# A second, packed table of powers for the outputs of a state-space mixer, stored by GpSimd beside the full one

## The chip, the cores and the metric

One core of one Trainium2 chip. The metric is device time in microseconds for one execution. The kernel before took 4363.01 us in the median of three runs (4361.12 to 4366.87).

## The reference, cut to what matters

Two blocks of a diffusion-style transformer run one after the other on 512 latent and 256 context tokens of width 1024, all in 32-bit floats. The last mixer is a diagonal state-space model over 128 groups of 16 channels with 64 complex states each, run in both directions:

```python
lam = lax.complex(lam_re, lam_im)
dt = jnp.exp(log_step)[:, None]
abar = jnp.exp(lam * dt)
bbar = ((abar - 1.0) / lam)[..., None] * bmat
...
h[t] = abar * h[t - 1] + bbar @ u[t]
y[t] = (c @ h[t]).real
```

The kernel works in chunks of 8 tokens. A chunk's outputs are what its inputs give inside the chunk (a Toeplitz block) plus the entering state times C times the powers 1 to 8 of `abar` in one direction, and the powers in the other order in the backward one. So C times nine powers of `abar` (0 to 8) is a table. The kernels (Toeplitz rows) need powers 0 to 7, the outputs need 1 to 8.

## The kernel before, in words

The whole network is one program of blocks. A block gives each engine its own stream of instructions, and ends when every engine has drained; the next block starts on all engines together. Weights come through a ring of two slots (`c.ring`), loaded by SP.

**The table routine.** `s5_tables` (line 2034) makes the tables for a range of the 16 blocks of channels, wholly on GpSimd, beside the work of other engines in three earlier stages: blocks 0 to 2 in the first attention (lines 941 and 3160), blocks 3 to 10 in the first product of the first feed-forward layer (`dense_seven`, line 360 on, called at 3174 to 3184), and blocks 11 to 15 in the window attention (line 3276). The call is the whole of GpSimd's stream in that block of the program, with its last waits on its own stores. Per block of channels it runs, in this order: six products for direction 0 of the input table, loads for direction 1 (`load_b`, lines 2061 and 2063), the real part of the power table (three products of 1152 columns, `times`, lines 2081 to 2083), its store (`keep_c`, line 2071), six products for direction 1, the store of the input table (line 2108), loads for the next block, a wait until the power table's store has landed, the other part of the power table into the same buffer, its store, six short products for a small table, its store (line 2118), and three loads (lines 2066 to 2068). Every product waits for the one it depends on. GpSimd issues all these transfers itself.

The power table of one block of channels is `[128, part 2, direction 2, pair 4, power 9, channel 16]`, 2304 floats per partition, kept in DRAM as `s5_c9`.

**The mixer.** In `s5_mixer` (line 2125) the rows of the input projection are turned through DRAM, `inputs` makes each chunk's contribution to the states, and `kernels` makes the Toeplitz rows for blocks 0 to 13 early. VectorE then scans the states of both halves of the blocks. After that comes a list of 18 turns, `turn`: the outputs of block 0, kernels 14, outputs 1, kernels 15, then outputs 2 to 15. Turn n uses half n % 2 of the ring, in which GpSimd has loaded the power table (`for_turn`, line 2278, 1152 KB) once turn n - 2 is done (line 2304 and after). After it GpSimd issues eight loads of Toeplitz rows (line 2319). `outputs` on TensorE multiplies 128 of the 144 columns of each of 16 pieces of the table by the entering states (line 2396), then adds the Toeplitz part (line 2403). ScalarE copies the states apart (`part_states`) and the results out, SP stores them, and SP and ScalarE load them back turned.

```python
for n, (kind, b) in enumerate(turn):
    if n >= 2:
        before, of = turn[n - 2]
        pool.wait_ge(y_done if before == "y" else k_done, of + 1)
        for_turn(n)
```

Of the kernel before, what the change touches and what calls it, by code (L numbers as in the profile page):

```python
# [2024 lines left out]
def s5_scratch(c):  # L2025

    dram = lambda name, *shape: c.nc.dram_tensor(name, shape, F32, kind="Internal").ap()
    c.s5 = {"fa": dram("s5_fa", S5_STEP, 2, 128, 128), "pc": dram("s5_pc", 16, 128, 160), "a8": dram("s5_a8", 128, 512),
            "b8": dram("s5_b8", 16, 128, 2048), "c9": dram("s5_c9", 16, 128, 2304), "fb": dram("s5_fb", 16, 128, 512),
            "us": dram("s5_us", 16, 128, T), "ys": dram("s5_ys", 16, 128, LAT), "e": dram("s5_e", 16, 128, 240),  # L2030
            "h": dram("s5_h", 128, KD * LAT), "u": dram("s5_u", 128, KD * LAT)}


def s5_tables(c, pool, spaces, first, end):

    nc = c.nc
    used = [0] * len(spaces)

    def take(*shape):

        n = int(np.prod(shape))
        i = next(i for i, x in enumerate(spaces) if used[i] + n <= x.shape[1])
        v = spaces[i][:, used[i]:used[i] + n]
        used[i] += n
        names = "abc"[:len(shape)]
        return v.rearrange(f"p ({' '.join(names)}) -> p {' '.join(names)}", **dict(zip(names[1:], shape[1:]))) if len(shape) > 1 else v
    bn, fa, b8 = take(2, 512), take(2, 512), take(2, 2, 512)
    prod = take(8, S5_POW, 16)  # L2050
    c9 = take(8, S5_POW, 16)
    cp, pc, bz, fb = take(2, 8, 16), take(160), take(2, 8, 32), take(2, 8, 32)
    tag = f"s5tab{first}_"
    in_b, in_c, made, b8_out, c9_out, fb_out = (c.sem(tag + n) for n in ("in_b", "in_c", "made", "b8_out", "c9_out", "fb_out"))
    tt = nc.gpsimd.tensor_tensor
    n = [0]

    def load_b(b, d):
        for part in range(2):
            rows = c.s5["fa"][:, part, 8 * b + 4 * d:8 * b + 4 * d + 4, :].rearrange("r a y -> r (a y)")  # L2060
            pool.dma_start(fa[:, part, :], rows.unsqueeze(1).broadcast_to([S5_STEP, 16, 512])).then_inc(in_b, 16)
            cols = c.ins["s5_bn"][b, :, 1024 * part + 512 * d:1024 * part + 512 * d + 512]
            pool.dma_start(bn[:, part, :], cols.unsqueeze(0).broadcast_to([S5_STEP, 16, 512])).then_inc(in_b, 16)

    def load_c(b):
        pool.dma_start(cp.rearrange("p a b c -> p (a b c)"), c.ins["s5_cp"][b]).then_inc(in_c, 16)
        pool.dma_start(pc, c.s5["pc"][b]).then_inc(in_c, 16)
        pool.dma_start(bz.rearrange("p a b c -> p (a b c)"), c.ins["s5_bz"][b]).then_inc(in_c, 16)

    def keep_c(b, part):  # L2070
        pool.dma_start(c.s5["c9"][b, :, 1152 * part:1152 * part + 1152], c9.rearrange("p a b c -> p (a b c)")).then_inc(c9_out, 16)

    def step(ins):

        ins.then_inc(made, 1)
        n[0] += 1
        pool.wait_ge(made, n[0])

    def times(out, tmp, re_, im_, a, b, sign):

        tt(out, re_, a, ALU.mult)  # L2081
        step(tt(tmp, im_, b, ALU.mult))  # L2082
        step(tt(out, out, tmp, ALU.add if sign > 0 else ALU.subtract))  # L2083
    def make_b(b, d):

        pool.wait_ge(in_b, 64 * (2 * (b - first) + d + 1))
        flat = prod.rearrange("p a b c -> p (a b c)")[:, 0:512]
        times(b8[:, 0, d, :], flat, bn[:, 0, :], bn[:, 1, :], fa[:, 0, :], fa[:, 1, :], -1)
        times(b8[:, 1, d, :], flat, bn[:, 0, :], bn[:, 1, :], fa[:, 1, :], fa[:, 0, :], 1)
    load_b(first, 0)  # L2090
    load_c(first)
    for b in range(first, end):
        done = b - first
        if done:
            pool.wait_ge(b8_out, 16 * done)
        make_b(b, 0)
        load_b(b, 1)
        pool.wait_ge(in_c, 48 * (done + 1))
        if done:
            pool.wait_ge(c9_out, 32 * done)  # L2100
            pool.wait_ge(fb_out, 16 * done)
        cb = lambda part: cp[:, part].unsqueeze(2).broadcast_to([128, 8, S5_POW, 16])
        pb = lambda part: (pc[:, 72 * part:72 * part + 72].rearrange("p (k e) -> p e k", e=8).unsqueeze(3)
                           .broadcast_to([128, 8, S5_POW, 16]))
        times(c9, prod, cb(0), cb(1), pb(0), pb(1), 1)
        keep_c(b, 0)
        make_b(b, 1)
        pool.dma_start(c.s5["b8"][b], b8.rearrange("p a d n -> p (a d n)")).then_inc(b8_out, 16)
        if b + 1 < end:
            load_b(b + 1, 0)  # L2110
        pool.wait_ge(c9_out, 32 * done + 16)
        times(c9, prod, cb(0), cb(1), pb(1), pb(0), -1)
        keep_c(b, 1)
        fp = lambda part: pc[:, 144 + 8 * part:152 + 8 * part].unsqueeze(2).broadcast_to([128, 8, 32])
        small = prod.rearrange("p a b c -> p (a b c)")[:, 0:256].rearrange("p (a b) -> p a b", a=8)
        times(fb[:, 0], small, bz[:, 0], bz[:, 1], fp(0), fp(1), -1)
        times(fb[:, 1], small, bz[:, 0], bz[:, 1], fp(1), fp(0), 1)
        pool.dma_start(c.s5["fb"][b], fb.rearrange("p a b c -> p (a b c)")).then_inc(fb_out, 16)
        if b + 1 < end:
            load_c(b + 1)  # L2120
    for sem, per in ((b8_out, 16), (c9_out, 32), (fb_out, 16)):
        pool.wait_ge(sem, per * (end - first))


def s5_mixer(c):
# [10 lines left out]
    nc = c.nc  # L2136
# [8 lines left out]
    b8 = [c.view(rest + 2048 * n, 2, 2, 8, 64) for n in range(2)]  # L2145
    toep = [c.view(rest + 1024 * n, 8, 128) for n in range(2)]
    fb = [c.view(rest + 2048 + 512 * n, 2, 2, 4, 32) for n in range(2)]
    band = [c.view(rest + 3072 + 240 * n, 240) for n in range(2)]
    yst = [c.view(rest + 3552 + 512 * n, 512) for n in range(2)]
    powers = lambda x: x.rearrange("p (a d q k) -> p a d q k", a=2, d=2, q=4)  # L2150
    c9 = [powers(c.ring[:, n, 0:2304]) for n in range(2)]
    free = c.hu[:, 0].rearrange("p a b -> p (a b)")
    c9_first = [powers(free[:, 2304 * n:2304 * n + 2304]) for n in range(2)]
    fb_first = [free[:, 4608 + 512 * n:5120 + 512 * n].rearrange("p (a d q n) -> p a d q n", a=2, d=2, q=4) for n in range(2)]
    band_first = [free[:, 5632 + 240 * n:5872 + 240 * n] for n in range(2)]
    NF = 14
    turn = [x for b in range(NB - NF) for x in (("y", b), ("k", NF + b))] + [("y", b) for b in range(NB - NF, NB)]
    place = {x: c9[n % 2] for n, x in enumerate(turn)} | {("k", b): c9_first[b % 2] for b in range(NF)}
    band_of = lambda b: (band_first if b < NF else band)[b % 2]
    fb_of = lambda b: (fb_first if b < NF else fb)[b % 2]  # L2160
    spot = lambda b: c.P[:, 2 * ((b // 2) % 2) + b % 2, 768:1008] if b < NF else bank(4 + b % 2)[:, 0:240]
# [18 lines left out]
    b8_in, c9_in, c9_first_in, fb_in, e_out, t_in, ys_out = (  # L2180
        [S(f"{w}{n}") for n in range(2)] for w in ("b8_in", "c9_in", "c9_first_in", "fb_in", "e_out", "t_in", "ys_out"))
# [26 lines left out]
    with nc.Block() as block:  # L2208
# [42 lines left out]
        def _(pool):  # L2251
# [23 lines left out]

            def for_turn(n):

                pool.dma_start(c9[n % 2].rearrange("p a d q k -> p (a d q k)"), c.s5["c9"][turn[n][1]]).then_inc(c9_in[n % 2], 16)
            load_b8(0)
            load_b8(1)  # L2280
            pool.wait_ge(spilled, 32)
# [20 lines left out]
# [3 lines that stand above are left out]
# [18 lines left out]
        def _(pe):  # L2323
# [60 lines left out]
            def outputs(b):  # L2384

                n = turn.index(("y", b))
                pe.wait_ge(c9_in[n % 2], 16 * (n // 2 + 1))
                if b >= 4:
                    pe.wait_ge(y_kept, b - 3)
                to = [bank(b % 4)[:, 2 * CL * q:2 * CL * (q + 1)] for q in range(4)]  # L2390
                for d in range(2):
                    pe.wait_ge(parted, 2 * b + d + 1)
                    for q in range(4):
                        for part in range(2):
                            of = 16 * (1 - d)
                            last = nc.tensor.matmul(to[q], place["y", b][:, part, d, q, of:of + 128],
                                                    apart[(2 * b + d) % 3][:, part, q].rearrange("p e s -> p (e s)"),
                                                    start=d == 0 and part == 0 and q == 0, stop=False, skip_group_check=True)
                    last.then_inc(apart_used, 1)
                pe.wait_ge(t_in[b % 2], 128 * (b // 2 + 1))  # L2400
                for q in range(4):
                    for e in range(2):
                        last = nc.tensor.matmul(to[q][:, CL * e:CL * (e + 1)], toep[b % 2][:, 2 * q + e, :], up[:, b, 2 * q + e, CX:CH],
                                                start=False, stop=q == 3 and e == 1, skip_group_check=True)
                last.then_inc(y_done, 1)
# [1012 lines left out]
```

## Time and profile before

| | |
|---|---|
| median of three runs | 4363.01 us |
| the profiled execution, time | 4374.75 us |
| the profiled execution, span | 4373.0 us |
| mean granted TensorE clock | 0.95 of full |
| TensorE / VectorE / ScalarE / GpSimd busy | 90 / 58 / 28 / 28% |
| DMA traffic | 532.69 MB, 122 GB/s |

The profiled execution took 11.7 us longer than the median. Busy shares are means over stages that have different limits. A busy TensorE is not TensorE at its peak. `q` behind an engine's name (POOLq) is its sequencer: branches, drains, semaphores and the issue of transfers. The time from issue to landing of a transfer is not part of the instruction's own duration.

### The profile page before, as it was taken

Reading aid. Unit: us, or ns where it says so; the run is one execution under the profiler, and the core shown is the slowest. Engines: PE = TensorE matmul, PEld = TensorE weight load, DVE = VectorE, ACT = ScalarE, POOL = GpSimd, SP = SyncE. Lnnn points to the kernel's source line nnn. Section 1 sums busy time; section 2 is a strip of 40 time slices with the busy share of each in tenths; the row PEclk is TensorE's granted clock in tenths of the full one; section 3 lists DMA queues with packets and bytes.
Section 4 is the critical chain, followed back from the end, with each engine's and each line's share of the span. In section 5 each row is a group of like instructions: output and inputs, shape, how many; then the busy total and the mean of one; then the engine's idle time right before and its main releaser. Section 6 shows DMA issues by size and latency. Waiting matters only on the chain. (4 is left out here: it accounts for less than half of the span.)

```text
span 4373.0 us, 53517 instructions
## 1 busy us (share of the span) xinstructions
PE 3922.7 (90%) x19818; PEld 2826.6 (65%) x19818; DVE 2536.2 (58%) x4524; ACT 1235.2 (28%) x2638; POOL 1214.4 (28%) x1480
## 2 busy tenths in 40 slices
PE   7899899989889777898989999989999789659998
PEld 4577455555445565777878885568755456658886
DVE  6634799982379885557678734245534309823353
ACT  3145311100212474662021102128611211341112
POOL 1174299950000068820000000059600011440000
PEclk9999999999999988999999999999999899889999
DMA  4542366651121066544345422124211276783221
GB/s 172 190 115 78 118 176 187 177 166 60 36 77 58 18 195 176 116 95 165 105 157 174 147 71 76 63 65 111 89 58 53 73 259 197 231 219 117 77 87 67
DMA packets 287391, 532.69 MB, mean 122 GB/s; under 512 B 176960, under 2 KB 184000, under 8 KB 262848
## 3 DMA queue, kind: packets, MB, share of 16 engines
q1 hardware_dynamic: 215872, 343.19, 24.2%
q0 software_dynamic: 53600, 181.04, 14.0%
q10 hardware_dynamic: 17696, 5.56, 0.6%
q8 instruction: 130, 2.13, 0.2%
q14 instruction: 93, 0.76, 0.1%
HBM read 429.55 MB, written 100.01 MB: 121 GB/s over the span
## 5 line engine op out<-in xcount | busy, mean ns | idle before, releaser
L417 PE MATMUL P<-hu,ring 128*128 128x384 f32 (+1 forms) x2448 | 746.3, 458 | 22.2 <-PEq L171 12.1
L417 PEld LDWEIGHTS P<-hu,ring 128*128 128x128 f32 x2448 | 466.8, 191 | 277.8 <-issue 25.6
L653 PE MATMUL P<-area,ring 128*128 128x256 f32 (+1 forms) x1880 | 493.9, 419 | 48.9 <-PEq L393 27.2
L653 PEld LDWEIGHTS P<-area,ring 128*128 128x128 f32 x1880 | 362.5, 194 | 169.7 <-issue 65.3
L417 PE MATMUL P<-area,ring 128*128 128x256 f32 (+1 forms) x1584 | 442.2, 431 | 3.6 <-DVE area L544 2.8
L873 POOL TENSOR_TENSOR fold<-mod,vec 128x16 f32<-128x16 f32 (+1 forms) x5 | 1.0, 206 | 1383.9 <-SPq L852 961.6
L417 PEld LDWEIGHTS P<-area,ring 128*128 128x128 f32 x1584 | 300.5, 190 | 127.6 <-issue 5.3
L653 PE MATMUL P<-area,hu 128*128 128x256 f32 (+1 forms) x1104 | 296.7, 423 | 0.0
L653 PEld LDWEIGHTS P<-area,hu 128*128 128x128 f32 x1104 | 209.8, 190 | 77.2
L2596 DVE SCALAR_TENSOR_TENSOR area<-area 128x1024 f32<-128x1024 f32 x122 | 220.4, 1807 | 19.1 <-ACT area L2672 17.0
L1092 DVE TENSOR_REDUCE stat<-P 128x1 f32<-128x512 f32 (+1 forms) x144 | 99.4, 690 | 151.2 <-PE P L1011 93.0
L2339 PE MATMUL P<-hu,ring 128*128 128x256 f32 (+1 forms) x512 | 169.3, 492 | 15.2 <-PEq L852 15.2
L2083 POOL TENSOR_TENSOR area<-area 128x512 f32<-128x512 f32 (+2 forms) x104 | 180.4, 1735 | 8.2
L1008 PE MATMUL P<-area 128*128 128x256 f32 (+2 forms) x480 | 167.7, 433 | 11.3 <-DMA area<-in_window_mask 5.9
L417 PE MATMUL P<-hu 128*128 128x384 f32 x504 | 170.6, 488 | 5.7 <-DVE hu L529 3.4
L2081 POOL TENSOR_TENSOR area<-area 128x512 f32<-128x512 f32 (+2 forms) x110 | 169.2, 1538 | 19.4 <-DMA area<-in_s_bn 15.7
L2082 POOL TENSOR_TENSOR area<-area 128x512 f32<-128x512 f32 (+2 forms) x104 | 157.4, 1514 | 0.0
L2339 PEld LDWEIGHTS P<-hu,ring 128*128 128x128 f32 x512 | 97.7, 192 | 84.7 <-issue 78.3
L1035 PE MATMUL P<-tmp,area 128*128 128x128 f32 x1152 | 152.4, 275 | 0.1
L879 POOL TENSOR_TENSOR tmp<-tmp 128x768 f32<-128x768 f32 (+1 forms) x6 | 9.3, 1542 | 488.5 <-ACT tmp L904 488.5
L417 PEld LDWEIGHTS P<-hu 128*128 128x128 f32 x504 | 95.0, 190 | 75.6 <-DVE hu L529 6.4
L3086 ACT ACTIVATE tmp<-P 128x768 f32<-128x768 f32 (+1 forms) x44 | 31.0, 704 | 395.2 <-DVE P L549 373.7
(457 smaller groups left out, 7218.6 us busy)
## 6 DMA issues: line engine op xcount, KB each, us to landing
ring<-in_w_ffn_in SPq DMA_DIRECT2D x44, 1024.0 KB, 4.8
area<-in_w_mod SPq DMA_DIRECT2D x69, 512.0 KB, 3.4
ring<-s_c POOLq DMA_DIRECT2D x18, 1152.0 KB, 9.8
stat<-in_w_mod SPq DMA_DIRECT2D x39, 512.0 KB, 3.4
s_c<-area POOLq DMA_DIRECT2D x32, 576.0 KB, 3.4
ring<-in_w_ffn_out SPq DMA_DIRECT2D x24, 704.0 KB, 4.0
area<-s_b POOLq DMA_DIRECT2D x16, 1024.0 KB, 5.4
hu<-s_c POOLq DMA_DIRECT2D x14, 1152.0 KB, 8.9
```

What stands on the lines that cost most here:

```text
L417: last = mm(to, col(a, k), b[:, k, :], start=fresh and k == 0, stop=k == q - 1, skip_group_check=True)
L653: last = mm(to, a[:, 128 * k:128 * k + 128], b[k], start=fresh and k == 0, stop=k == q - 1, skip_group_check=True)
L879: nc.gpsimd.tensor_tensor(sq[0], sq[0], sq[1], ALU.add).then_inc(s["paired"], 1)
L1008: last = nc.tensor.matmul(S[n % 2][:, a:b], q(i, j, t), k(i, j, key, key + b - a), start=True, stop=rope is None and not (edges and key < ...
L1035: last = nc.tensor.matmul(O[n % 2], v(i, j, key), probT[:, n % 2, b * 128:b * 128 + 128], start=b == 0, stop=b == len(tiles) - 1)
L1092: nc.vector.reduce_max(small[:, n % slots, 0:1], scores(n), AX.X).then_inc(sem["top"], 1)
L2081: tt(out, re_, a, ALU.mult)
L2082: step(tt(tmp, im_, b, ALU.mult))
L2083: step(tt(out, out, tmp, ALU.add if sign > 0 else ALU.subtract))
L2339: last = nc.tensor.matmul(c.P[:, 2 * (g % 2) + j, a:b], c.ring[:, s, (j * KD + k) * 128:(j * KD + k + 1) * 128], c.u[:, k, a:b], start=k = ...
L2596: return c.nc.vector.scalar_tensor_tensor(out=junk, in0=weights, scalar=1.0, in1=c.view(CONDS, 2, D)[:, cc % 2, :], op0=ALU.mult, op1=ALU. ...
L3086: return None if j else act_fn(split_tile(tmp[:, 0:w].unsqueeze(1)), split(ps, n), ACT.Silu)
```

## The change

`s5_tables` keeps storing the full table and now stores a second one, `s5_c8`, beside it: for each part, direction 0's powers 1 to 8 and direction 1's powers 0 to 7, as `[128, part, direction, 512]`. That is two more stores after each of the two present ones, each 256 KB, read from the table's buffer as four pieces of 128 floats per partition, written as 512 floats in a row. The semaphore of these stores counts 96 per block in place of 32, in all waits on it. In the mixer the turns of kind "y" load the packed table (1024 KB, 2048 floats per partition) in place of the full one (1152 KB); the turns of kind "k" and the early kernels still load the full one. The matmul of line 2396 takes all 128 columns of a piece in place of 128 of 144.

```diff
--- before.py
+++ after.py
@@ -2026,7 +2026,7 @@
 
     dram = lambda name, *shape: c.nc.dram_tensor(name, shape, F32, kind="Internal").ap()
     c.s5 = {"fa": dram("s5_fa", S5_STEP, 2, 128, 128), "pc": dram("s5_pc", 16, 128, 160), "a8": dram("s5_a8", 128, 512),
-            "b8": dram("s5_b8", 16, 128, 2048), "c9": dram("s5_c9", 16, 128, 2304), "fb": dram("s5_fb", 16, 128, 512),
+            "b8": dram("s5_b8", 16, 128, 2048), "c9": dram("s5_c9", 16, 128, 2304), "c8": dram("s5_c8", 16, 128, 2, 2, 512), "fb": dram("s5_fb", 16, 128, 512),
             "us": dram("s5_us", 16, 128, T), "ys": dram("s5_ys", 16, 128, LAT), "e": dram("s5_e", 16, 128, 240),
             "h": dram("s5_h", 128, KD * LAT), "u": dram("s5_u", 128, KD * LAT)}
 
@@ -2069,6 +2069,9 @@
 
     def keep_c(b, part):
         pool.dma_start(c.s5["c9"][b, :, 1152 * part:1152 * part + 1152], c9.rearrange("p a b c -> p (a b c)")).then_inc(c9_out, 16)
+        for d in range(2):
+            later = c9[:, 4 * d:4 * d + 4, 1 - d:9 - d, :].rearrange("p a b c -> p a (b c)")
+            pool.dma_start(c.s5["c8"][b, :, part, d, :].rearrange("p (a n) -> p a n", a=4), later).then_inc(c9_out, 16)
 
     def step(ins):
 
@@ -2097,7 +2100,7 @@
         load_b(b, 1)
         pool.wait_ge(in_c, 48 * (done + 1))
         if done:
-            pool.wait_ge(c9_out, 32 * done)
+            pool.wait_ge(c9_out, 96 * done)
             pool.wait_ge(fb_out, 16 * done)
         cb = lambda part: cp[:, part].unsqueeze(2).broadcast_to([128, 8, S5_POW, 16])
         pb = lambda part: (pc[:, 72 * part:72 * part + 72].rearrange("p (k e) -> p e k", e=8).unsqueeze(3)
@@ -2108,7 +2111,7 @@
         pool.dma_start(c.s5["b8"][b], b8.rearrange("p a d n -> p (a d n)")).then_inc(b8_out, 16)
         if b + 1 < end:
             load_b(b + 1, 0)
-        pool.wait_ge(c9_out, 32 * done + 16)
+        pool.wait_ge(c9_out, 96 * done + 48)
         times(c9, prod, cb(0), cb(1), pb(1), pb(0), -1)
         keep_c(b, 1)
         fp = lambda part: pc[:, 144 + 8 * part:152 + 8 * part].unsqueeze(2).broadcast_to([128, 8, 32])
@@ -2118,7 +2121,7 @@
         pool.dma_start(c.s5["fb"][b], fb.rearrange("p a b c -> p (a b c)")).then_inc(fb_out, 16)
         if b + 1 < end:
             load_c(b + 1)
-    for sem, per in ((b8_out, 16), (c9_out, 32), (fb_out, 16)):
+    for sem, per in ((b8_out, 16), (c9_out, 96), (fb_out, 16)):
         pool.wait_ge(sem, per * (end - first))
 
 
@@ -2149,13 +2152,14 @@
     yst = [c.view(rest + 3552 + 512 * n, 512) for n in range(2)]
     powers = lambda x: x.rearrange("p (a d q k) -> p a d q k", a=2, d=2, q=4)
     c9 = [powers(c.ring[:, n, 0:2304]) for n in range(2)]
+    c8 = [powers(c.ring[:, n, 0:2048]) for n in range(2)]
     free = c.hu[:, 0].rearrange("p a b -> p (a b)")
     c9_first = [powers(free[:, 2304 * n:2304 * n + 2304]) for n in range(2)]
     fb_first = [free[:, 4608 + 512 * n:5120 + 512 * n].rearrange("p (a d q n) -> p a d q n", a=2, d=2, q=4) for n in range(2)]
     band_first = [free[:, 5632 + 240 * n:5872 + 240 * n] for n in range(2)]
     NF = 14
     turn = [x for b in range(NB - NF) for x in (("y", b), ("k", NF + b))] + [("y", b) for b in range(NB - NF, NB)]
-    place = {x: c9[n % 2] for n, x in enumerate(turn)} | {("k", b): c9_first[b % 2] for b in range(NF)}
+    place = {x: (c8 if x[0] == "y" else c9)[n % 2] for n, x in enumerate(turn)} | {("k", b): c9_first[b % 2] for b in range(NF)}
     band_of = lambda b: (band_first if b < NF else band)[b % 2]
     fb_of = lambda b: (fb_first if b < NF else fb)[b % 2]
     spot = lambda b: c.P[:, 2 * ((b // 2) % 2) + b % 2, 768:1008] if b < NF else bank(4 + b % 2)[:, 0:240]
@@ -2275,7 +2279,9 @@
 
             def for_turn(n):
 
-                pool.dma_start(c9[n % 2].rearrange("p a d q k -> p (a d q k)"), c.s5["c9"][turn[n][1]]).then_inc(c9_in[n % 2], 16)
+                kind, b = turn[n]
+                table = c.s5["c8"][b].rearrange("p a d n -> p (a d n)") if kind == "y" else c.s5["c9"][b]
+                pool.dma_start(place[turn[n]].rearrange("p a d q k -> p (a d q k)"), table).then_inc(c9_in[n % 2], 16)
             load_b8(0)
             load_b8(1)
             pool.wait_ge(spilled, 32)
@@ -2392,8 +2398,7 @@
                     pe.wait_ge(parted, 2 * b + d + 1)
                     for q in range(4):
                         for part in range(2):
-                            of = 16 * (1 - d)
-                            last = nc.tensor.matmul(to[q], place["y", b][:, part, d, q, of:of + 128],
+                            last = nc.tensor.matmul(to[q], place["y", b][:, part, d, q, :],
                                                     apart[(2 * b + d) % 3][:, part, q].rearrange("p e s -> p (e s)"),
                                                     start=d == 0 and part == 0 and q == 0, stop=False, skip_group_check=True)
                     last.then_inc(apart_used, 1)
```

## Rows read from the trace of the kernel before

**Rows 1.** Windows; columns: us, busy (instructions) per engine, PEclk, DMA, GB/s.
```profile
517.00:949.00 432.00, 406.81 (x1240) 236.29 (x1240) 393.13 (x321) 56.47 (x103) 392.29 (x312) 0.98 0.62 183
...
3747.00:3923.00 176.00, 116.80 (x1013) 113.56 (x1008) 96.21 (x202) 68.10 (x116) 88.76 (x152) 0.84 0.81 229
```

**Rows 2.** End of the feed-forward stage, line 393; ns min/median/max, start.
```profile
L393 DVEq COMPARE_BRANCH  x1: 47/47/47, 940.3 to 940.3; - x1
...
L393 POOLq COMPARE_BRANCH  x1: 38/38/38, 944.5 to 944.5; - x1
L393 POOLq DRAIN  x1: 4627/4627/4627, 944.7 to 944.7; - x1
...
L393 PEldq EVENT_SEMAPHORE  x1: 51/51/51, 949.5 to 949.5; - x1
```

**Rows 3.** Waits from 940 to 950 us: us in total, times, longest.
```profile
DVE area L725 <- PEq L393: 9.3, 1, 9.3
```

**Rows 4.** End of the window attention, line 975.
```profile
L975 POOLq DRAIN  x1: 6179/6179/6179, 3138.9 to 3138.9; - x1
...
L975 DVEq DRAIN  x1: 325/325/325, 3145.6 to 3145.6; - x1
```

**Rows 5.** End of the first attention, line 975.
```profile
L975 POOLq DRAIN  x1: 3732/3732/3732, 381.6 to 381.6; - x1
...
L975 DVEq DRAIN  x1: 325/325/325, 416.4 to 416.4; - x1
```

**Rows 6.** Waits in the output turns, 3747 to 3923 us.
```profile
POOL ring L2278 <- PE P L2403: 61.0, 13, 18.6
...
PE P L2396 <- ACT tmp L2427: 29.0, 6, 16.9
PE P L2396 <- DMA ring<-s_c: 24.8, 9, 5.5
```

**Rows 7.** Line 2071, the present stores of the table.
```profile
L2071 POOL DMA_DIRECT2D s_c<-area x32: 600/621/627, 268.2 to 3131.2; - x32
...
DMA to landing us min/median/max: 3.1/3.4/6.6
```

**Rows 8.** Other transfers of GpSimd: lines 1447 and 2256.
```profile
L1447 POOL DMA_DIRECT2D hu<-gdn_xa x8: 565/566/575, 1623.4 to 1659.8; - x8
...
L2256 POOL DMA_DIRECT2D area<-s_b x16: 527/528/579, 3485.5 to 3749.3; - x16
```

**Rows 9.** GpSimd in the feed-forward stage: waits, then in order of time.
```profile
POOL area L2081 <- DMA area<-in_s_bn: 10.3, 4, 6.5
...
528.57 3.00 POOL L2081 TENSOR_TENSOR area<-area 128x512 f32<-128x512 f32 x1 [6.49 <-DMA area<-in_s_bn]
...
553.13 0.62 POOL L2071 DMA_DIRECT2D s_c<-area  x1 [0.30 <-POOL area L2083]
555.45 2.12 POOL L2081 TENSOR_TENSOR area<-area 128x512 f32<-128x512 f32 x1 [1.70 <-DMA area<-in_s_bn]
...
569.58 2.33 POOL L2081 TENSOR_TENSOR area<-area 128x1152 f32<-128x1152 f32 x1
```

**Rows 10.** GpSimd's products of 512 columns: later stages, then first attention.
```profile
L2083 POOL TENSOR_TENSOR area<-area 128x512 f32<-128x512 f32 x52 | 79.3, 1525 | 4.1
...
L2083 POOL TENSOR_TENSOR hu<-hu 128x512 f32<-128x512 f32 x12 | 15.2, 1270 | 0.9
```

**Rows 11.** Line 2118, the store of the small table, 256 KB.
```profile
DMA to landing us min/median/max: 2.4/2.4/4.3
```

**Rows 12.** Line 2278; 3720 to 3762; page: KB, median us to landing.
```profile
DMA to landing us min/median/max: 6.4/9.8/12.6
...
area<-s_b POOLq DMA_DIRECT2D x6, 1024.0 KB, 6.4
ring<-s_c POOLq DMA_DIRECT2D x2, 1152.0 KB, 9.2
...
ring<-in_w_s_in SPq DMA_DIRECT2D x8, 1024.0 KB, 8.9
```

## The prediction

> **What bounds the kernel now.** I read the page first. No engine is full over the span and the chain of the end is only the last layer norm, so the stages must be read one by one. GpSimd and ScalarE have the smallest shares of the span, which says nothing of the stretches where GpSimd makes the tables: in the longest it is busy 392.3 of 432 us [rows 1].
>
> Then I read what ends each stage that runs the table routine, by the drains and branches that close a block. The feed-forward stage (eight tables): VectorE reaches its branch at 940.3, GpSimd at 944.5, GpSimd's drain then takes 4.63 us, and all engines go on at 949.5 [rows 2]. VectorE waited 9.3 us there for that block's end [rows 3]. So **GpSimd ends this stage**. The window attention (five tables): GpSimd's drain runs from 3138.9 for 6.18 us, to 3145.1; VectorE's from 3145.6 to 3145.9 [rows 4]. GpSimd has 0.8 us of slack. The first attention (three tables): GpSimd is through at 381.6 + 3.7 = 385.3, the block closes after VectorE's drain at 416.4 [rows 5], so about 31 us of slack.
>
> Last, the output part of the state-space mixer. TensorE waits there 24.8 us for the power table and 29.0 us for ScalarE's state copies [rows 6]; a table load is issued when the outputs two turns before are done, and GpSimd waits 61.0 us for those [rows 6]. The DMA engines are 81% busy there [rows 1].
>
> **The change, part by part.**
>
> *Four more stores per table, issued by GpSimd.* The present two stores cost 0.62 us each on its queue [rows 7]. The new ones carry 256 KB each, but a row is read as four pieces of 512 B, 512 pieces in all; no GpSimd transfer of before has so many. The nearest rows: a load of 128 pieces takes 0.528 us, one of 192 (line 1447: 32 rows by 6 by 128 B) 0.566 [rows 8], and the present store of 128 rows 0.621 [rows 7]; the count hardly shows. Lower bound: 0.53 us. Upper bound: if the whole 0.566 us went by pieces, 0.566 x 512 / 192 = 1.51 us. I take 0.62, since a store with as many rows is the nearest in kind.
> Whether VectorE stretches an issue: the 32 present stores took 0.600 to 0.627 us [rows 7], also those beside a VectorE that was 393 of 432 us busy [rows 1]. GpSimd's products are stretched there, a 512-column one from 1.27 up to 3.00 us [rows 9, 10], the issues are not. If they were, by the same factor, one would cost 1.46 us (rival 2).
> The Trainium skill (page SBUF — State Buffer, section SBUF: two separate sides) says that GpSimd can't write the descriptors of its transfers while VectorE runs an operation in a two-port mode, and gives about 3.1 us in place of 0.62 for such a transfer; taken as the cost of each of 52 issues that would be an estimate of some +160 us. The trace does not agree for this kernel's stores.
>
> *Feed-forward stage:* 8 x 4 x 0.62 = 19.8 us more on the engine that ends the stage. Part is absorbed: GpSimd waits 10.3 us in four places for the loads of the next product, 6.5 of it once at the start, before any store [rows 9]. The other three, 3.8 us together, come after the first store (the one shown, 1.70 us, begins at 553.75 [rows 9]); two issues ahead of each take away at most 1.24 us each. I take 3. The loads waited for are ahead of the stores in their queue, so the stores don't delay them. And the added time runs after VectorE has ended, where GpSimd's products are quicker: 1.27 us for 512 columns in the first attention, 1.53 in the mean later [rows 10]. The last 20 us of 432 gain some 1.5. Result: 19.8 - 3 - 1.5 = +15.3.
>
> *Window attention:* 5 x 4 x 0.62 = 12.4, less 0.8 of slack: +11.6. There TensorE now stands idle before its next block, and its first products may run at a lower granted clock; 0 to 3 us, I take 1. *First attention:* 3 x 4 x 0.62 = 7.4 us inside 31: nothing. If that cover were gone it would be 7.4.
>
> *The waits on the stores.* After the part-0 stores GpSimd needs the buffer back for part 1. Between lie six products, one store and four loads, 554 to 569.6 in the block shown [rows 9]; the present store lands in 3.4, 6.6 at most [rows 7], and two more of 256 KB at 2.4 to 4.3 each [rows 11] still fit. The second wait has as much cover. What stands behind it, if it is late, is the whole rest of the block. Priced at nothing. The final wait of each call is on the last store of the small table, issued after the new ones; at most 1 us, taken as nothing.
>
> *DMA traffic.* 64 stores of 256 KB, 16.8 MB, 13.6 of them in the two stages that count. Engines that wait for weights there don't end the stage. Nothing.
>
> *Output turns.* 16 of 18 loads shrink from 1152 to 1024 KB. A load lands in 9.8 us in the median [rows 12]. At an equal rate a ninth goes, 1.1 us. Two loads are in flight for two turns, so a turn gains half of that where the table is waited for: about 3 us over outputs 2 to 7; I put 1 for outputs 8 to 15, where the 29.0 us for ScalarE [rows 6] mostly fall. The store of outputs and its way back, for which ScalarE waits, shares the same engines. I take -4; bounds: 0, and what 16 x 128 KB take at the 229 GB/s of the stretch [rows 1], 9 us. The first two tables were loaded early and gain nothing. The matmuls read the same 128 columns: nothing. What is late next is ScalarE's chain of copies.
>
> *Sum:* 15.3 + 11.6 + 1 - 4 = **+24 us**. The profiled execution took 4374.75 (span 4373.0) and would take 4398.7; the median of the runs is 4363.01, 11.7 less than the profiled one, and I carry the same difference over: **4387**.
>
> **The rivals.**
> 1. *The issue goes by pieces.* Then 1.51 instead of 0.62: 48.3 - 3.8 + 30.2 - 0.8 + 1 - 4 = +71, 4434. For it: nothing in the trace has 512 pieces on this queue. Against: 128 and 192 pieces differ by 38 ns, and a present store of 128 takes more than either [rows 7, 8]. It decides if an issue passes 1 us.
> 2. *VectorE stretches the issues* of the feed-forward stage, where it is busiest, to 1.46: 46.7 - 3.8 + 11.6 + 1 - 4 = +51, 4414. For it: the products are stretched. Against: no present store is [rows 7]. (Beside this stands the rule of the Trainium skill's page SBUF — State Buffer, section SBUF: two separate sides.)
> 3. *Most comes back.* Issues at 0.53: 17.0 - 3.8 - 1.5 + 10.6 - 0.8 = 21.5, and the outputs gain their full 9 and the two stage ends, whose drains differ between 3.7 and 6.2 us [rows 4, 5], end 4 earlier together: +8.5, 4371, at the edge of no change.
> 4. *Faster.* The long rows themselves slow the table load, and a load of 1024 KB lands in 5 to 6 us: the other table, of that size, lands in 6.4 where this one takes 9.2 [rows 12]. Place: the output turns, where TensorE's 24.8 us of table waits go, and ScalarE's 29.0 by a third because the stores of outputs find the engines free: -34.5. It decides if that passes the +28 of the table stages: 4363 + 27.9 - 34.5 = 4356. Against: where the engines are busy a 1024 KB load of weights takes 8.9 [rows 12] too, and the fastest table load took 6.4 [rows 12].
> 5. *It doesn't do what it says.* The ring half is no smaller a target, and the same number of loads run; if the landing depends on the number of rows and not on bytes, the outputs gain nothing: +28, 4391. It is inside the forecast's range.
>
> **How the numbers follow.** Forecast with rival 5: 0.73. Rival 1: 0.10. Rival 2: 0.03. Rival 3: 0.09. Rival 4: 0.05. 0.2% is 8.7 us, about what a measurement can tell from no change. Slower takes the forecast and rivals 1 and 2, 0.86; same rival 3, 0.09; faster rival 4, 0.05. Range: the low terms (rival 3 without its earlier ends) give +12.5, so 4375, and I set 4374; upwards the forecast's own bounds (nothing absorbed, clock 3, outputs 0) give +34, 4397, and I go on to rival 2 and an issue of about 1 us, 4414, which holds half of rival 1. Left out: rivals 3 and 4 and half of 1, 0.19.
>
> **What would show it.** Right: four more GpSimd issues of about 0.62 us per table; blocks of the table routine about 2.5 us longer; VectorE's wait at the end of the feed-forward stage up from 9.3 to about 25 us, and some 12 us at the end of the window attention; table loads of 1024 KB landing near 8.7 us. Wrong: an issue near or above 1 us, GpSimd waiting for its own stores, or the feed-forward stage ended by VectorE.

## The result, and the profile after

The changed kernel takes 4394.45 us (median of 3 runs, 4392.08 to 4395.68) against 4363.01: ratio 1.0069 [1.0056, 1.0083], slower. Run again later, beside the kernel before on the same chip, it took 4381.78 (6 runs) against 4360.44 (26 runs): 1.0051 [1.0033, 1.0069], or +21.3 us. The first comparison gave +31.4; what lies between the two is taken up below.

The profile page of the changed kernel, its top and the transfers:

```profile
PE 3923.0 (89%) x19818; PEld 2829.5 (64%) x19818; DVE 2503.0 (57%) x4524; ACT 1237.5 (28%) x2638; POOL 1258.9 (29%) x1544
...
q0 software_dynamic: 58720, 195.73, 14.7%
...
HBM read 427.45 MB, written 116.79 MB: 124 GB/s over the span
```

GpSimd has 64 instructions more and is busy 44.5 us longer than before. TensorE's work is the same. So what is lost is time in which the other engines wait, and the places to look are the ends of stages. First the end of the feed-forward stage, changed kernel (duration min/median/max in ns, then the start):

```profile
L393 DVEq COMPARE_BRANCH  x1: 47/47/47, 932.9 to 932.9; - x1
...
L393 POOLq COMPARE_BRANCH  x1: 38/38/38, 961.3 to 961.3; - x1
L393 POOLq DRAIN  x1: 1284/1284/1284, 961.5 to 961.5; - x1
...
L393 PEldq EVENT_SEMAPHORE  x1: 51/51/51, 963.0 to 963.0; - x1
...
who waited for it (us, times):
  PE P L653: 35.7, 1
  DVE area L725: 30.2, 1
```

Beside [rows 2]: GpSimd reaches its branch 16.8 us later, VectorE 7.4 us earlier, and VectorE's wait of 9.3 us [rows 3] has become 30.2. GpSimd's drain, in return, takes 1.28 us instead of 4.63. Two windows show what was done in the feed-forward stage and in the output turns (columns as in [rows 1]), and the groups of GpSimd in the first (busy, mean ns of one, idle before):

```profile
517.00:963.00 446.00, 403.99 (x1240) 237.22 (x1240) 359.83 (x321) 57.80 (x102) 413.28 (x344) 0.95 0.65 196
3767.00:3943.00 176.00, 125.03 (x1092) 121.69 (x1092) 102.05 (x214) 69.70 (x119) 89.10 (x152) 0.82 0.80 224
```

```profile
L2086 POOL TENSOR_TENSOR area<-area 128x512 f32<-128x512 f32 (+2 forms) x64 | 117.2, 1831 | 5.0
L2085 POOL TENSOR_TENSOR area<-area 128x512 f32<-128x512 f32 (+2 forms) x64 | 108.6, 1696 | 0.0
L2084 POOL TENSOR_TENSOR area<-area 128x512 f32<-128x512 f32 (+2 forms) x64 | 95.6, 1493 | 9.2 <-DMA area<-in_s_bn 6.9
L2074 POOL DMA_DIRECT2D s_c<-area x32 | 24.6, 774 | 1.6 <-issue 1.6
```

GpSimd is busy 413.3 us against 392.3 [rows 1], +21.0. The 32 new issues are 24.6 of it; the products (121.5 + 102.7 + 100.4 before, 117.2 + 108.6 + 95.6 after) give 3.2 back. Its wait for in_s_bn falls from 10.3 [rows 9] to 6.9. Counted from the stage's own start, GpSimd's branch comes 17.5 us later, the drain is 3.3 shorter, and the stage 14.1 longer. VectorE runs the same 321 instructions in 359.8 us instead of 393.1, and that is no chance: every kernel with the added stores in this stage shows 360 to 366, every kernel without them there 381 to 394.

Between GpSimd's last issue and its branch stands one more wait, for the landing of its last store (line 2118 before, 2121 after). In the first profile of the kernel before, that store took 4.3 us to land:

```profile
L2118 POOL DMA_DIRECT2D s_fb<-area x1: 602/602/602, 940.1 to 940.1; - x1
...
DMA to landing us min/median/max: 4.3/4.3/4.3
```

In e0_before, after and e10_after it takes 2.3. So 2 us of the difference from one profile to another come from this one landing: by the pair before and after the stage grows by 14.1 us, by the pair e0_before and e10_after by 16.0.

The end of the window attention, changed kernel:

```profile
L975 DVEq DRAIN  x1: 325/325/325, 3158.6 to 3158.6; - x1
L975 POOLq COMPARE_BRANCH  x1: 32/32/32, 3167.5 to 3167.5; - x1
L975 POOLq DRAIN  x1: 4390/4390/4390, 3167.6 to 3167.6; - x1
...
L975 PEldq EVENT_SEMAPHORE  x1: 51/51/51, 3172.2 to 3172.2; - x1
...
  PE P L417: 13.7, 1
  DVE area L528: 13.4, 1
```

In [rows 4] VectorE's drain came last by 0.8 us; now GpSimd is the last by 13, and TensorE and VectorE wait 13.7 and 13.4 us for the block where they waited for none. In the first attention GpSimd's drain ends at 395.4 and VectorE's starts at 415.7: 20 us of the 31 of slack [rows 5] are left, and the stage stays at 178.6 us.

The new stores and the old ones, changed kernel, lines 2074 and 2071:

```profile
L2074 POOL DMA_DIRECT2D s_c<-area x64: 757/762/798, 268.9 to 3159.9; - x64
...
DMA to landing us min/median/max: 2.7/4.2/6.9
```

```profile
L2071 POOL DMA_DIRECT2D s_c<-area x32: 607/616/622, 268.3 to 3158.5; - x32
```

And GpSimd in order of time, at the place of [rows 9]:

```profile
552.49 0.62 POOL L2071 DMA_DIRECT2D s_c<-area  x1 [0.30 <-POOL area L2086]
553.09 1.54 POOL L2074 DMA_DIRECT2D s_c<-area  x2
555.55 1.37 POOL L2084 TENSOR_TENSOR area<-area 128x512 f32<-128x512 f32 x1 [0.92 <-DMA area<-in_s_bn]
...
568.95 2.29 POOL L2084 TENSOR_TENSOR area<-area 128x1152 f32<-128x1152 f32 x1
```

The wait for in_s_bn was 1.70 and is 0.92: 0.78 us of the issues was absorbed there. The product at 568.95, which first needs the three stores to have landed, follows the issue before it without a wait.

The output turns, waits in the stretch 3766 to 3943 us, and the page's row of the table loads:

```profile
POOL ring L2284 <- PE P L2408: 52.9, 12, 13.3
...
PE P L2401 <- DMA ring<-s_c: 21.6, 7, 5.4
PE P L2401 <- ACT tmp L2432: 20.8, 6, 10.4
```

```profile
ring<-s_c POOLq DMA_DIRECT2D x16, 1024.0 KB, 8.5
```

Against [rows 6]: 24.8 for the table has become 21.6, 29.0 for ScalarE 20.8. The unchanged kernel's second profile, though, shows 26.1 and 19.7 (e0_before, below), so one pair of profiles doesn't say what the change did to ScalarE's part. Against [rows 12]: a load lands in 8.5 us instead of 9.2 to 9.8.

**By stage.** The length of each stage, from one block's end to the next, for every kernel that ran (us; one profiled execution each; the other stages differ by up to 2.6 us):

| kernel | first attention | feed-forward | gated-delta heads | window attention | mixer to its end | end |
|---|---|---|---|---|---|---|
| before | 178.6 | 432.1 | 447.8 | 237.7 | 453.8 | 4372.9 |
| e0_before | 178.4 | 430.6 | 446.7 | 237.8 | 447.6 | 4364.6 |
| after | 178.6 | 446.2 | 446.2 | 250.9 | 446.4 | 4392.6 |
| e10_after | 178.4 | 446.6 | 442.7 | 250.8 | 437.1 | 4376.5 |
| e1_stores_only | 178.6 | 446.7 | 440.1 | 250.5 | 447.6 | 4382.3 |
| e2_load_only | 178.7 | 430.6 | 445.7 | 237.8 | 437.0 | 4352.1 |
| e8_sync_packs | 178.6 | 431.2 | 447.9 | 238.3 | 440.5 | 4358.7 |
| e9_packs_and_one_load | 178.4 | 430.0 | 442.2 | 237.8 | 440.2 | 4351.2 |
| e6_whole_rows | 178.4 | 442.4 | 439.7 | 244.7 | 448.4 | 4375.6 |
| e4_stores_window | 178.5 | 431.9 | 442.7 | 250.8 | 454.1 | 4380.3 |

The window attention repeats to 0.6 us among kernels with the same GpSimd code, the feed-forward stage to 0.6 with the added stores and to 1.5 without them, where the last store's landing differs. The gated-delta heads, which the change doesn't touch, go from 439.7 to 447.9 without order. The mixer falls into two groups: with loads of 1152 KB 447.6 to 454.1, mean 450.3 (five kernels); with loads of 1024 KB 437.0 to 446.4, mean 440.2 (five). So the change costs 14.1 to 16.0 and 13.0 to 13.2, by the pair of profiles taken, and gives back about 10: +17 to +19 from the stages, beside the +21.3 of the second comparison. Of the 10, 7.4 lie behind the first product of an output turn (from there to the mixer's end 171.3 us in the mean of the five with full loads, 163.9 with packed ones). The other 2.7 lie ahead of it, where that product comes between 275.0 and 281.2 us into the mixer, in the changed kernel itself last of all; whether they belong to the change stays open.

### The profile page after: what moved, and what is told of

It is laid out like the page before. It is cut to its first block and busy times, and to the rows that moved or that the text cites. A ratio compares the mean times of both kernels' runs of the same rounds, so it can differ in the third digit from the quotient of the medians.

```text
span 4392.7 us, 53581 instructions
## 1 busy us (share of the span) xinstructions
PE 3923.0 (89%) x19818; PEld 2829.5 (64%) x19818; DVE 2503.0 (57%) x4524; ACT 1237.5 (28%) x2638; POOL 1258.9 (29%) x1544
## 2 busy tenths in 40 slices
DMA packets 292512, 547.38 MB, mean 125 GB/s; under 512 B 177984, under 2 KB 185024, under 8 KB 267968
## 3 DMA queue, kind: packets, MB, share of 16 engines
q0 software_dynamic: 58720, 195.73, 14.7%
## 5 line engine op out<-in xcount | busy, mean ns | idle before, releaser
L417 PE MATMUL P<-hu,ring 128*128 128x384 f32 (+1 forms) x2448 | 747.8, 459 | 35.1 <-PEq L975 13.7
L2601 DVE SCALAR_TENSOR_TENSOR area<-area 128x1024 f32<-128x1024 f32 x122 | 211.7, 1735 | 19.1 <-ACT area L2677 16.9
L2345 PE MATMUL P<-hu,ring 128*128 128x256 f32 (+1 forms) x512 | 169.3, 492 | 15.2 <-PEq L852 15.2
L2084 POOL TENSOR_TENSOR area<-area 128x512 f32<-128x512 f32 (+2 forms) x110 | 164.1, 1491 | 16.3 <-DMA area<-in_s_bn 12.6
L466 ACT ACTIVATE tmp<-P 128x384 f32<-128x384 f32 (+1 forms) x153 | 67.9, 447 | 304.0 <-PE P L417 303.9
L1035 PEld LDWEIGHTS P<-tmp,area 128*128 128x128 f32 x1152 | 140.0, 192 | 0.4 <-ACT tmp L1066 0.4
```

The costliest lines, as they stand in the source:

```text
L417: last = mm(to, col(a, k), b[:, k, :], start=fresh and k == 0, stop=k == q - 1, skip_group_check=True)
L466: copy = lambda o, i: nc.scalar.activation(o, i, ACT.Copy)
L1035: last = nc.tensor.matmul(O[n % 2], v(i, j, key), probT[:, n % 2, b * 128:b * 128 + 128], start=b == 0, stop=b == len(tiles) - 1)
L2345: last = nc.tensor.matmul(c.P[:, 2 * (g % 2) + j, a:b], c.ring[:, s, (j * KD + k) * 128:(j * KD + k + 1) * 128], c.u[:, k, a:b], start=k = ...
L2601: return c.nc.vector.scalar_tensor_tensor(out=junk, in0=weights, scalar=1.0, in1=c.view(CONDS, 2, D)[:, cc % 2, :], op0=ALU.mult, op1=ALU. ...
```

## The experiments

The theory: GpSimd's queue ends two of the three stages, so its added issues go straight onto the path, and the output turns give a part back. The rivals: the 16.8 MB written more are what costs; an issue goes by its pieces; the smaller loads gain nothing.

**e0_before.** The kernel before, unchanged, as a measure of what no change looks like.

> The kernel before, unchanged, profiled once more. Its first profiled execution took 11.7 us longer than the median of its runs, the changed kernel's none longer. If GpSimd's drain at the end of a table stage is what differs between executions (4.63 us at the feed-forward stage in the first profile, 1.28 us in the changed kernel's), this profile shows another drain there, and a total that moves with it by a few us. If the drain is fixed by the program, it is again 4.6 us and the total spread lies elsewhere.

Measured: 0.9998 [0.9988, 1.0009], 4363.13 us. GpSimd's drain at the end of the feed-forward stage is again 4.627 us, so what differs between executions lies elsewhere. With ten runs and more on each side a ratio is known to 0.1%; the three runs of the first comparison of the change can't be read as finely.

**e1_stores_only.** The stores stay, the outputs load the full table.

```diff
-    place = {x: (c8 if x[0] == "y" else c9)[n % 2] for n, x in enumerate(turn)} | ...
+    place = {x: c9[n % 2] for n, x in enumerate(turn)} | ...
...
-                table = c.s5["c8"][b].rearrange("p a d n -> p (a d n)") if kind == "y" else c.s5["c9"][b]
+                table = c.s5["c9"][b]
```

> The 64 added stores stay, but the outputs load the full table of 1152 KB as before. By my theory the stores alone cost what the two table stages grew by in the profile, 14.1 + 13.2 = 27 us, and the outputs give nothing back: 27 to 38 us slower than before, and slower than the changed kernel by the 7 us that its outputs gained. By the rival, in which the packed loads give nothing outside the profiled execution, it equals the changed kernel, +31 us.

Measured: 1.0050 [1.0037, 1.0064], 4385.58 us, +23.3. Feed-forward 446.7 and window attention 250.5, as after the change; mixer 447.6, as before it. The whole is less than the 27 to 38 us expected, and only 2 us above the +21.3 of the changed kernel, where 7 were expected: inside the intervals of the two ratios. This pair doesn't show what the loads give; the next kernel does.

**e2_load_only.** No second table; the outputs load the first 2048 floats of each full row. The products of the outputs then take other columns than they should; the instructions are the same.

```diff
-        for d in range(2):
-            later = c9[:, 4 * d:4 * d + 4, 1 - d:9 - d, :].rearrange("p a b c -> p a (b c)")
-            pool.dma_start(...)
...
-                table = c.s5["c8"][b].rearrange("p a d n -> p (a d n)") if kind == "y" else c.s5["c9"][b]
+                table = c.s5["c9"][b][:, 0:2048] if kind == "y" else c.s5["c9"][b]
```

> No second table is stored; the outputs load the first 2048 of 2304 floats of each row of the full table (the matmuls then read other columns than they should, so the outputs are not those of the model). By my theory this is the gain alone: 4 to 9 us faster than before, with table loads that land in about 8.5 us. By the rival, that the loads give nothing, no difference, within 3 us.

Measured: 0.9979 [0.9969, 0.9989], 4352.83 us, -9.5. The loads' gain is real, and by its interval (4.8 to 13.5 us) more than the 4 that the prediction took. Its output turns, beside those of e0_before, both waits of TensorE; first e2_load_only:

```profile
PE P L2398 <- DMA ring<-s_c: 20.5, 9, 5.6
PE P L2398 <- ACT tmp L2429: 16.6, 4, 8.8
```

```profile
PE P L2396 <- DMA ring<-s_c: 26.1, 8, 6.0
...
PE P L2396 <- ACT tmp L2427: 19.7, 6, 5.7
```

The two waits fall by 8.7 us together, 5.6 of it at the table. This is one pair of profiles; the means over all kernels stand further below.

**e8_sync_packs.** The second table is made, but by SyncE, which copies it out of the stored full table: blocks 0 to 10 during the window attention, one block's copies landed before the next block's are issued; blocks 11 to 15 in the next stage (att_z). GpSimd issues nothing new, and the DMA engines move more than in the change, since the copies also read.

```diff
+def pack(c, sp, b, sem):
+    for part in range(2):
+        for d in range(2):
+            src = c.s5["c9"][b, :, 1152 * part + 576 * d:1152 * part + 576 * d + 576].rearrange("p (a n) -> p a n", a=4)
+            sp.dma_start(c.s5["c8"][b, :, part, d, :].rearrange("p (a n) -> p a n", a=4),
+                         src[:, :, 16 * (1 - d):16 * (1 - d) + 128]).then_inc(sem, 16)
...
-        for d in range(2):
-            later = c9[:, 4 * d:4 * d + 4, 1 - d:9 - d, :].rearrange("p a b c -> p a (b c)")
-            pool.dma_start(...)
```

> The second table is not stored by GpSimd but copied from the full one in DRAM by SP: blocks 0 to 10 one after the other in the window attention, where SP issues nothing else after the mask, blocks 11 to 15 at the second group of the product after it. By my theory the cost is GpSimd's queue alone, so this should end like the load-only kernel: 3 to 9 us faster than before, and some 35 us faster than the changed kernel. By the rival that the DMA traffic of the second table makes the cost, it stays 10 us or more slower than before. The five late copies may hold up a weight load: 0 to 10 us.

Measured: 0.9982 [0.9972, 0.9991], 4356.77 us, -5.5. The copies in the trace:

```profile
L2043 SPq DMA_DIRECT2D s_c<-s_c x64: 530/637/1728, 2908.3 to 3162.4; - x64
...
DMA to landing us min/median/max: 3.4/5.1/12.5
```

Window attention 238.3 (before 237.7): with 44 of the 64 copies in that one stage, its DMA share goes from 0.39 to 0.57 and the stage takes 0.6 us more. So in this stage the bytes don't cost, the queue that issues them does. No kernel moved the bytes of the second table in the feed-forward stage without GpSimd's issues; what speaks for the same cause there is that GpSimd ends the stage, its own account above, and e6_whole_rows below.

**e10_after.** The changed kernel again, beside 26 runs of the kernel before on the same chip.

> The changed kernel again, beside the others on one chip. Stage by stage its profile against the kernel before says +15 in the feed-forward stage, +13 in the window attention and -4 to -8 in the mixer, in all +20 to +24; the first comparison, of three runs each, said +31. If the sum of the stages is right, the ratio comes out at 1.0045 to 1.0055. If a part is hidden from the stage comparison, it is 1.007 again.

Measured: 1.0051 [1.0033, 1.0069], 4381.78 us, +21.3.

**e6_whole_rows.** Stores of the same number and size, but each row is one piece of 2 KB, so 128 pieces instead of 512. The second table then holds other columns, and the outputs load the full one.

```diff
+        flat = c9.rearrange("p a b c -> p (a b c)")
         for d in range(2):
-            later = c9[:, 4 * d:4 * d + 4, 1 - d:9 - d, :].rearrange("p a b c -> p a (b c)")
-            pool.dma_start(c.s5["c8"][b, :, part, d, :].rearrange("p (a n) -> p a n", a=4), later).then_inc(c9_out, 16)
+            pool.dma_start(c.s5["c8"][b, :, part, d, :], flat[:, 512 * d:512 * d + 512]).then_inc(c9_out, 16)
```

> As many stores of the same size as in the change, but each reads 512 floats in a row per partition (other data than the second table needs), 128 pieces of 2 KB in place of 512 of 512 B; the outputs load the full table. If the issue costs by pieces, an issue takes 0.62 us in place of 0.76 and the feed-forward stage ends about 32 x 0.14 = 4.5 us earlier than with the change's stores (446 us), at 442; the window attention 2.8 us earlier. If the price is the instruction's, 0.76 stays. By a theory that DMA traffic makes the cost, the stages stay at 446 and 251, since the bytes are the same. Whole: +16 to +20 us over before.

Measured: 1.0035 [1.0023, 1.0047], 4377.06 us, +16.6.

```profile
L2074 POOL DMA_DIRECT2D s_c<-area x64: 539/544/580, 269.0 to 3146.2; - x64
```

0.762 - 0.544 = 0.218 us for 384 pieces, 0.57 ns a piece, on about half a microsecond that an issue takes in any case. The transfers themselves are as many: this kernel and e1_stores_only both count 292512 DMA packets and 549.48 MB. With the same traffic and cheaper issues the feed-forward stage is 4.3 us shorter than there and the window attention 5.8, so in both stages the cost follows the issues. The issues are cheaper than expected (0.54, not 0.62) and the window attention falls to 244.7, twice as far as expected, the feed-forward stage only to 442.4, which the drains explain (below).

**e4_stores_window.** The added stores only in the call of the window attention, as in the change; none in the other two; the outputs load the full table, of which the second holds only the last five blocks.

```diff
     def keep_c(b, part):
         pool.dma_start(...)
+        if not (first == 11):
+            return
         for d in range(2):
```

> The added stores are made for blocks 11 to 15 only, in the window attention; the outputs load the full table. Window attention 250.7 us in place of 237.8, all other stages as before: +13 us in all, and GpSimd's drain there 4.4 us, not 6.2, while the drains of the two earlier table stages stay at 3.7 and 4.6 if each goes with the code of its own block.

Measured: 1.0034 [1.0022, 1.0046], 4376.22 us, +15.8. The window attention alone takes its full 13 us, the feed-forward stage 431.9, nothing. The prices of the two stages are separate and add up.

**e9_packs_and_one_load.** e8_sync_packs, and besides two small inputs of each table are laid out as one array, which GpSimd loads with one issue instead of two.

```diff
-        pool.dma_start(cp.rearrange("p a b c -> p (a b c)"), c.ins["s5_cp"][b]).then_inc(in_c, 16)
+        pool.dma_start(cz, c.ins["s5_cz"][b]).then_inc(in_c, 16)
...
-        pool.dma_start(bz.rearrange("p a b c -> p (a b c)"), c.ins["s5_bz"][b]).then_inc(in_c, 16)
...
-        pool.wait_ge(in_c, 48 * (done + 1))
+        pool.wait_ge(in_c, 32 * (done + 1))
```

> As the kernel in which SP copies the second table, and two of GpSimd's loads per table (inputs of 128 and 256 KB) are made one, so each table has one issue of 0.54 us less. If GpSimd's queue sets the end of the feed-forward stage, where VectorE is ready some 9 us earlier, eight issues less shorten it by 4 us and the whole comes to 4352, 0.1% under the kernel without the merge. If the stage's end goes with something else, nothing changes. In the window attention 0.8 us or less.

Measured: 0.9968 [0.9954, 0.9981], 4347.04 us. It beats both kernels. How much of it is the merged load is open: its interval and that of e8_sync_packs overlap, and the feed-forward stage is shorter by 1.2 us only (430.0 against 431.2), where eight issues of 0.55 us would give 4.4. GpSimd's last issue of that stage does come 3.0 us sooner, counted from the stage's start, and the drain is 0.5 us shorter, but the store issued there takes 2.4 us longer to land, and the block waits for it. First e9_packs_and_one_load, then e8_sync_packs:

```profile
L2131 POOL DMA_DIRECT2D s_fb<-area x1: 602/602/602, 936.7 to 936.7; - x1
...
DMA to landing us min/median/max: 5.1/5.1/5.1
```

```profile
L2131 POOL DMA_DIRECT2D s_fb<-area x1: 602/602/602, 940.1 to 940.1; - x1
...
DMA to landing us min/median/max: 2.7/2.7/2.7
```

## Why the prediction was right, and where its terms were off

The direction and the places were right: GpSimd ends two of the three table stages (e1_stores_only and e4_stores_window put the loss there and nowhere else), the first attention hides its share, the output turns give a part back, and no wait on the stores appeared. 4387 lies between the two measurements of the change, 4382 and 4394. Term by term:

- *An issue of 0.62 us.* It was 0.762, 0.774 in the mean of the feed-forward stage. "The count hardly shows" was the step that failed: 128 and 192 pieces differ by 0.038 us [rows 8], which is 0.59 ns a piece, and that slope over 512 pieces gives 0.528 + 384 x 0.59 ns = 0.755. The two rows held the answer; I took the nearest in kind in place of the slope. The 0.62 of the present stores holds something besides the count of rows, and at least part of it goes with the place, since each is issued right behind a product: in e6_whole_rows the small table's store (line 2121), 128 rows of 2 KB like those of line 2074 there but issued right behind a product, takes 0.586 us where line 2074 takes 0.544. Rival 1, all by pieces, 1.51, was wrong too: half a microsecond doesn't depend on the count.
- *Feed-forward, +15.3.* 24.6 for the issues (19.8 predicted), 3.4 less at the waits for in_s_bn (3 predicted; 0.5 of the 3.4 is at the wait ahead of the first store, so 2.9 was absorbed), 3.2 from quicker products (1.5 predicted), and 3.3 from a shorter drain (not foreseen) leave 14.7; with the last store's landing, 2 us shorter, and small items the other way it is +14.1 in the first pair of profiles, +16.0 from e0_before to e10_after. That 15.3 lies between the two is in part luck: the dearer issue (+4.8) and the shorter drain (-3.3) cancelled.
- *Window attention, +11.6 and 1 for the clock.* Twenty issues and what goes with them move GpSimd's branch by 15.8 us, the drain is 1.8 shorter, 0.8 was slack: +13.2. The stage after it (att_z) takes 150.6 us with and without the change, so the clock term, for which the prediction had no row, is nothing. Here too the sum of 12.6 came out near 13.2 because a dearer issue (15.2 us for twenty in place of 12.4) met a shorter drain.
- *Waits on stores, 0.* Right. They land in 2.7 to 6.9 us, and in the block shown the product that needs them comes 14 us behind.
- *Output turns, -4.* They gave about -7 (means of five against five, from the first output product to the mixer's end; -10 for the whole mixer), and e2_load_only ran 9.5 faster [4.8 to 13.5]. So the term was about half of what came. What it sized too low is the part of ScalarE's state copies, which it met with 1 us for outputs 8 to 15: in the means of the same five and five kernels TensorE's wait for the table falls from 24.8 to 22.1 us and that for ScalarE's copies from 23.7 to 19.1. This is weaker than the other terms: a mixer with the same loads differs by up to 9.4 us from kernel to kernel, the wait for ScalarE by up to 10.
- *The offset of 11.7 us.* Profiled 4374.75 against a median of 4363.01 before; after, the profiled execution was the median, 4394.45. The offset was the luck of one execution; what made 4387 come out is that the predicted growth of 24 was set on the median, which a profiled execution can miss by 12 us. The profiled total grew by 19.7, the medians by 31.4 and, measured again, by 21.3.

The rivals. *VectorE stretches the issues* fell: 64 issues lie between 757 and 798 ns, also beside a VectorE that is 360 of 446 us busy. The Trainium skill's rule (page SBUF — State Buffer, section SBUF: two separate sides), by which such an issue would wait for VectorE's two-port operations, is not shown here. It isn't refuted either, and the prediction's sentence that the trace doesn't agree with it went too far: VectorE's time in this stage is nearly all in operations with two tensor inputs, such as line 2601's 116.4 us of SCALAR_TENSOR_TENSOR, and no view says in which mode an operation ran. *Faster* fell: the loads land in 8.5 to 9.1 us, not 5 to 6. *Most comes back* had two true parts, the shorter drains, for which it allowed 4 us and which gave 3.3 + 1.8, and a larger gain of the outputs; its cheap issue was wrong. *It doesn't do what it says* fell with e2_load_only.

Why the first comparison gave +31 and the second +21 stays open. The two table stages give +27 to +29 in every pair of profiles; the gated-delta heads and the mixer spread by 7 to 9 us without relation to the change, and three runs on each side don't average that out. That this is the whole of it is not shown: the changed kernel's three first runs (4392 to 4396) all lie above its six later ones (4378 to 4389).

## What to carry to other kernels

Before adding instructions to an engine that is a third busy, look at who closes each block: here a queue with 28% of the span ended two stages, and most of what was put there was paid: 24.6 us of issues cost 14 to 16, 15.2 us cost 13, while 9 us in the stage that VectorE closed cost nothing. The same table, copied by transfers issued from SyncE, cost the stage that took them less than 1 us. A DMA issue of GpSimd here costs 0.54 us at 128 pieces and 0.57 ns for each piece more, and a store of the same size right behind a product took 0.04 more; where two rows of before differ in the count alone, use their slope. And compare stage by stage: the touched stages repeated to 1.5 us, while the 26 runs of the kernel before lie between 4348 and 4373.

## What was not expected of the hardware

GpSimd's drain at the end of a block in which it made tables takes from 1.28 to 6.59 us. It repeats to 0.01 us wherever GpSimd's instructions in the block are the same, and doesn't follow how many there are. At the end of the feed-forward stage, first e10_after, then e6_whole_rows:

```profile
L393 POOLq COMPARE_BRANCH  x1: 38/38/38, 959.3 to 959.3; - x1
L393 POOLq DRAIN  x1: 1284/1284/1284, 959.5 to 959.5; - x1
```

```profile
L393 POOLq COMPARE_BRANCH  x1: 38/38/38, 952.4 to 952.4; - x1
L393 POOLq DRAIN  x1: 6587/6587/6587, 952.6 to 952.6; - x1
```

The cheaper issues bring e6_whole_rows to its branch some 9.5 us earlier, counted from each stage's start, and the drain takes 5.3 of that back: that is why the stage gained 4 us and not 9. In the window attention it goes the other way: there the branch comes 3.7 us earlier and the drain is shorter too, 1.93 us in e6_whole_rows instead of 4.39, together the 6 us that the stage gained:

```profile
L975 POOLq DRAIN  x1: 1932/1932/1932, 3153.7 to 3153.7; - x1
```

In e4_stores_window only the window attention has the added stores, and only its drain is that of the change:

```profile
L975 POOLq DRAIN  x1: 4387/4387/4387, 3148.2 to 3148.2; - x1
```

4.387 there and 4.390 in the changed kernel, against 6.179 [rows 4]. What the drain waits for isn't settled; no run here tests it.
